# Row factor at the head's output, low weight halves behind the next head's maxima, and filler matmuls in the last expert quad

## The reference, cut to what matters

```python
p = jax.nn.softmax(s, axis=-1)
a = p[:, :, 0] - lam * p[:, :, 1]
o = einsum('bhqk,bkhe->bqhe', a, v)
o = o * lax.rsqrt(jnp.mean(o * o, axis=-1, keepdims=True) + LN_EPS)
```

```python
hid = jax.nn.silu(jnp.einsum('td,edf->tef', t, w1[gi])) * jnp.einsum('td,edf->tef', t, w3[gi])
hid = hid * gate[:, gi, :, None]
out = out + jnp.einsum('tef,efd->td', hid, w2[gi])
```

## Time and profile before

| what | value |
|---|---|
| median of 3 runs | 1187.81 us (1185.96 to 1189.49) |
| profiled execution, its own time | 1190.7 us |
| span of its core | 1188.9 us |
| mean granted clock | 0.974 |
| TensorE matmul busy | 1118.6 us, 94% |
| VectorE busy | 699.5 us, 59% |
| ScalarE busy | 556.3 us, 47% |
| HBM read | 281.87 MB, 239 GB/s over the span |

### The profile page before, as it was taken

How to read it: one execution, slowest core, us unless ns; L and a number is a source line. 1 busy time by engine, 2 the same in 40 slices (tenths; PEclk the granted TensorE clock), 3 DMA queues, 4 the chain that set the end, 5 groups by cost and what they waited for, 6 DMA issues and landing times. The chain is left out here.

```text
span 1188.9 us, 17973 instructions
## 1 busy us (share of the span) xinstructions
PE 1118.6 (94%) x7231; PEld 898.8 (76%) x7231; DVE 699.5 (59%) x1041; ACT 556.3 (47%) x953; POOL 52.4 (4%) x94
## 2 busy tenths in 40 slices
PE   7998899999999999999998999999999999889676
PEld 5987688888789987888887878988887866546333
DVE  3487867778766667778778626745456643312112
ACT  4567556556545646555655424345543322213112
POOL 5000000010000000010000000000000000000000
PEclk9999999999999999999998999999999989979988
DMA  9943378888755333888873652455647799999995
GB/s 273 290 168 104 107 224 295 292 280 292 244 163 191 108 117 130 321 293 275 285 262 100 137 177 72 142 206 180 209 139 262 280 374 369 389 398 386 417 416 225
DMA packets 126510, 285.17 MB, mean 240 GB/s; under 512 B 12222, under 2 KB 72891, under 8 KB 118369
## 3 DMA queue, kind: packets, MB, share of 16 engines
q1 hardware_dynamic: 116512, 249.29, 59.9%
q0 software_dynamic: 9920, 34.80, 9.1%
HBM read 281.87 MB, written 2.20 MB: 239 GB/s over the span
## 5 line engine op out<-in xcount | busy, mean ns | idle before, releaser
L2000 DVE TENSOR_TENSOR w_lo<-ring,w_hi 128x1024 fp32r<-128x1024 f32 (+1 forms) x272 | 320.3, 1212 | 101.1 <-ACT w_hi L1507 91.7
L1507 ACT ACTIVATE w_hi<-ring 128x1024 fp32r<-128x1024 f32 (+1 forms) x272 | 277.0, 1047 | 102.8 <-PE acc L680 77.2
L678 PE MATMUL acc<-w_hi,x_two 128*128 128x512 f32 (+2 forms) x320 | 128.5, 402 | 5.3 <-DVE x_two L1985 4.1
L680 PE MATMUL acc<-w_hi,x_two 128*128 128x512 f32 (+2 forms) x320 | 123.4, 386 | 0.0
L679 PE MATMUL acc<-w_lo,x_two 128*128 128x512 f32 (+2 forms) x320 | 123.3, 385 | 0.0
L678 PE MATMUL pp<-x_two,w_hi 128*128 128x256 f32 x384 | 112.5, 293 | 0.0
L679 PE MATMUL pp<-x_two,w_hi 128*128 128x256 f32 x384 | 108.5, 283 | 0.0
L680 PE MATMUL pp<-x_two,w_lo 128*128 128x256 f32 x384 | 108.5, 283 | 0.0
L678 PE MATMUL acc<-w_hi,hid_hi 128*128 128x512 f32 x256 | 99.8, 390 | 0.0
L680 PE MATMUL acc<-w_hi,hid_lo 128*128 128x512 f32 x256 | 99.6, 389 | 0.0
L679 PE MATMUL acc<-w_lo,hid_hi 128*128 128x512 f32 x256 | 99.6, 389 | 0.0
(11 more groups left out here) (397 smaller groups left out, 2135.4 us busy)
## 6 DMA issues: line engine op xcount, KB each, us to landing
ring<-in_w_up_dram SPq DMA_DIRECT2D x32, 1024.0 KB, 5.7
ring<-in_w_down_dram SPq DMA_DIRECT2D x32, 1024.0 KB, 6.6
exp_ring<-in_w_dram SPq DMA_DIRECT2D x32, 1024.0 KB, 11.3
stage<-in_w_ada_dram POOLq DMA_DIRECT2D x48, 512.0 KB, 6.2
ring<-in_w_in_dram SPq DMA_DIRECT2D x24, 1024.0 KB, 5.3
ring<-in_w_in_a_dram SPq DMA_DIRECT2D x12, 1024.0 KB, 14.2
mod<-in_w_dram SPq DMA_DIRECT2D x19, 512.0 KB, 12.9
ring<-in_w_kv_shared_dram SPq DMA_DIRECT2D x8, 1024.0 KB, 6.2
```

The source lines that it names most:

```text
L678: pe.matmul(out, lhs[0], rhs[0], start=start, stop=False)
L680: return pe.matmul(out, lhs[1], rhs[0], start=False, stop=stop)
L1507: act.activation(shaped(high_half(b, k), raw), raw, ACT.Copy).then_inc(S["hi_ready"], 1)
L2000: dve.tensor_tensor(shaped(low_half(b, k), raw), raw, shaped(high_half(b, k), raw), ALU.subtract).then_inc(S["lo_ready"], 1)
```

## The change

In the last quad TensorE runs five filler matmuls between `up(0)` and the wait for w3. In layer 0 the first map's factor 1/sum is no longer multiplied into the weights: the second map's factor becomes minus lambda times its inverse sum times the first map's sum, and ScalarE's `out` multiplies by the first map's inverse sum, in two instructions (one for each query tile, each with its factor column) where one stood. In both attention layers each `low` of the loop moves behind the next `first`: the low parts of blocks 9 and 11 of a layer move from the end of an iteration to behind the `first` of the next one's even head, those of blocks 8, 10 and 12 from ahead of `first(2i-1)` to behind it. `heads_stat(0, 4)` keeps its place right behind `second(4)`, where `low(12)` no longer stands ahead of it.

```diff
@@ TensorE, experts
                     up(0, lambda e, cols: w1_slots[:, 4 * (s % 2) + e, cols], between=i * 2 + 2).then_inc(S["w1_used"], 1)
+                    if s + 1 == QUADS:
+                        busy(5, turn_bank)
                     pe.wait_ge(w3_in[s % 2], (80 if s % 2 else 64) * (s // 2 + 1))
@@ ScalarE, out(c), layer 0
-                        act.activation(o_tm[:, :, 128 * c:128 * c + 128], head_banks(c)[:, :, 384:512], ACT.Copy)\
-                            .then_inc(S["o_done"], 1)
+                        for q in range(QT):
+                            last = act.activation(o_tm[:, q, 128 * c:128 * c + 128], head_bank(c, q)[:, 384:512],
+                                                  ACT.Identity, scale=rsum[:, c % 2, 2 * q:2 * q + 1])
+                        last.then_inc(S["o_done"], 1)
@@ VectorE, second(c), layer 0
                     for q in range(QT):
                         r1 = rsum[:, b, 2 * q + 1:2 * q + 2]
-                        last = dve.tensor_tensor(r1, r1, lam_s[:, 0:1], ALU.mult)
-                    link(last)
-                    for q in range(QT):
-                        cols = slice(0, 128) if q == 0 else slice(128, 384)
-                        last = dve.tensor_scalar(prob[:, b, 0, cols], prob[:, b, 0, cols],
-                                                 rsum[:, b, 2 * q:2 * q + 1], None, ALU.mult)
+                        last = dve.scalar_tensor_tensor(r1, r1, lam_s[:, 0:1], esum[:, b, 2 * q:2 * q + 1],
+                                                        ALU.mult, ALU.mult)
                     link(last)
@@ VectorE, loop over i of attention
                     first(2 * i - 2)
                     if i >= 2:
+                        low(bl + 5 + 2 * i)
                         out(2 * i - 3)
                     second(2 * i - 2)
-                    low(bl + 6 + 2 * i)
                     if i == 3:
                         heads_stat(0, 4)
                     first(2 * i - 1)
+                    low(bl + 6 + 2 * i)
                     if i == 3:
                         heads_scale(0, 4, 1)
                     keys(i)
                     if i < 3:
                         out(2 * i - 2)
                         second(2 * i - 1)
-                        low(bl + 7 + 2 * i)
                 second(5)
```

## The result

The changed kernel took 1180.95 us (median of 11 runs, 1176.18 to 1183.58) beside 1187.81 for the kernel before (11 runs): 6.9 us less by the medians. The ratio is 0.9938, with a 95% interval from 0.9917 to 0.9960, which is 7.4 us less (4.7 to 9.9). The profiled execution took 1179.81 us with a span of 1178.0, against 1190.7 and 1188.9.

The account below looks back on a forecast made before the run. TensorE, busy for 94% of the span, was taken as the bound, with its stops and half-clock stretches as the losses. Layer 0's 1.8, layer 1's 0 and the fillers' 2.7 us made 4.5 off 1187.81: 1183.3 us, range 1181.0 to 1187.5.

Parts of the forecast that it names:

- The swap: Layer 0, low behind first: scores of head 3 come 1.57 us earlier, those of head 5 2.36 us earlier.
- any wait for w_lo: Sign of being wrong: TensorE waiting anywhere for a low half of the weights.
- rival 4: Blocks 8 to 12, both layers: low halves too late, 1.5 us slower at 0.6 each, 1189.3 us; chance 0.05.
- What is late next: Layer 0: statistics wait for squares, TensorE's stop before o_tm's transposes grows to 2.7 us; turn of head 5 2.03 earlier.
- The end of layer 0: From the turn of head 5 on: ScalarE's tail gives back 0.23 of 2.03 us, leaving 1.8.
- Layer 0's term: Layer 0's attention: 1.8 us gained, with nothing counted for a change in its half-clock stretch.
- rival 1: Layer 0 also loses its half-clock stretch, 1.7 us more: 6.2 us gained, 1181.6 us; chance 0.15.
- Rival 2: Layer 0: the 2.7 us stop brings longer half clock, 1.6 us more; gain 2.9, 1184.9 us; chance 0.15.
- The fillers: Last chunk of the experts: fillers cost nothing in the w3 wait; up(1) at full clock gains 2.7 us.
- Rival 3: One gain does not arrive: layer 0 alone, 1186.0 us, or the fillers' 2.7 alone, 1185.1 us; chance 0.20.
- Layer 1: Layer 1's attention: moved low halves stay hidden, by 1.2 us at block 9; gain and loss 0.
- The sum: Whole kernel: layer 0, layer 1 and the fillers together, 4.5 us less, 1183.3 us.

Follow-up runs that it names:

- e13: The kernel before, unchanged, one more single execution; 1185.2 us.
- e15: The kernel before, unchanged, another single execution; 1182.5 us.
- e12: The changed kernel with ScalarE's squares of head 3 moved ahead of its high halves of block 12; 0.9908 of the kernel before, 1176.95 us.
- e1: The kernel before with the five last-quad fillers alone; ratio 1.0005 to the kernel before.
- e4: The changed kernel without the fillers; ratio 0.9974 to the kernel before.
- e10: The kernel before with the five fillers alone, measured a second time; ratio 0.9971 to the kernel before.
- after: The first profiled execution of the changed kernel; 1179.81 us.
- e7: The changed kernel with the five fillers in the last two quads instead of only the last; ratio 0.9939 to the kernel before.
- e8: The changed kernel again, unaltered, timed in the set of the other experiments; ratio 0.9929 to the kernel before.
- e9: The changed kernel with five filler calls on TensorE ahead of layer 1's loop; ratio 0.9993 to the kernel before.
- e11: The changed kernel without the fillers, measured a second time; ratio 0.9953 to the kernel before.
- e14: The changed kernel, unaltered, one more single execution; 1181.1 us.
- e16: The changed kernel, unaltered, another single execution; 1186.9 us.
- e18: The changed kernel, unaltered, measured a third time; ratio 0.9954 to the kernel before.
- e3: The kernel before with only the row factor moved to the output copy; ratio 0.9974 to the kernel before.
- e17: The changed kernel with head 3's squares ahead of block 12's high halves, measured a second time; ratio 0.9919 to the kernel before.

## Why the prediction was right or wrong

**The swap: right.** 1.57 us before the scores of head 3 were forecast, 1.57 came; the shift at the scores of head 5 was to be 2.36 and was 2.37. The two output copies took 0.61 us (0.65 taken). No wait for a low half appeared where the low halves were moved. The one of 2.7 us ahead of the loop has no moved `low` ahead of it, and e13 and e15, of the kernel before, have it too (1.3 and 1.1 us); so that sign of being wrong ("any wait for w_lo") was drawn too wide, and rival 4 is out.

**What is late next: right.** VectorE's wait for the squares 1.89 (2.1 forecast), TensorE's stop 2.64 (2.7), the turn of head 5 2.05 earlier (2.03). e12 shows the cause by removing it. The last figure is so near because two small misses cancel: the scaling started 0.1 us sooner than forecast, and `second(5)` took 1.25 us, not 1.15. Its two products with one operation more took 0.35 us where the old ones took 0.23: the upper bound of my 0 to 0.1, not the nothing that I took.

**The end of layer 0: mis-sized.** I kept 1.8 of 2.03. At equal clock it is 2.24 (89.60 for e1, 87.36 for e4): the turn of head 7 came 0.8 sooner and ScalarE's tail gave 0.6 back, by the wait [1.4 <-issue] that was 0.7.

**Layer 0's term, with the half-clock stretch left as it is: the step that failed.** The term was 1.8 us of work, and "the half-clock stretch I leave as it is" put the clock's share at 0, from one execution. In the profiled pair it was not 0: layer 0 had its stretch before and none after, and gave 3.5 us where I had 1.8. But the stretch is part of an execution and not of the kernel: the order of before runs without it twice in six, the changed kernel with it three times in five. Over the profiles of the two layouts layer 0 took 90.3 us on average in the old one (before, e1, e10, e13, e15) and 88.0 in the changed one (after, e4, e7, e8, e9, e11, e14, e16, e18). Of these 2.4 us 2.2 are the work at full clock; half clock cost 0.75 us on average in the old layout and 0.6 in the new. So on average the 0 was nearly right, and the work was what the term had too small, by 0.4; that is a part of the miss, and the sum below has the rest as far as it is known. One stretch costs 1.25 us (90.85 against 89.60 in the order of before), where rival 1 put 1.7. Rival 1 (6.2 us, 1181.6) came nearest to the measured median by luck: e8, e16 and e18 fell to half clock in that place. Rival 2's mechanism was seen as well, two stretches on end (6.8 us) in e8 and e18, though layer 0 still took less there than before (89.2 and 89.8 us). The rule from the Trainium skill that I set beside it (TensorE: Matmul & The Clock Gate, "Part 4: PE-mode transpose": transposes do not count as busy time like matmuls) is not settled: after a stop of 2.6 us the same transposes ran at full clock in some executions and at half in others, in after and in e8 for instance.

**The fillers: right in kind, over by a part in the rows.** 2.7 was the profiled execution's price. Seven profiles without fillers took 16.5 to 19.2 us from up(1) to the end, 18.2 on average, the thirteen with fillers 16.5 each: 1.8. I priced one execution and not the spread. Rival 3 (no gain from them) is out: e1 and e10 together lie 2.3 us below the kernel before (standard error 0.6). e7 adds that they arrive only behind the last weights.

**Layer 1: right**, 41.03 us from the scores of head 1 to the transposes of o_tm in every profile.

**The sum.** The stages of single executions give 2.4 + 1.8 = 4.2 us, nearly the 4.5 of the forecast. The timed runs give more: the three measurements of the change lie at 0.9938, 0.9929 and 0.9954, and over all timed runs the mean span fell from 1185.65 (96 runs, standard error 0.3) to 1179.85 (29 runs, 0.5), by 5.8 us, standard error 0.6. On the forecast's scale that is 1182.0, inside the range; that the first median fell below its end is in part the draw of eleven runs, and in part that the range ended only 0.6 us below rival 1.

The granted clock that every timed run has on record says more than the stages. Within the runs of one kernel a clock lower by 0.001 goes with a longer span: by 0.7 us in the kernel before, 0.9 in the changed one, 0.5 to 0.8 in the others with twelve runs or more but for e3's 1.1. The last column is worked out: the work at full clock by the rows, and 0.8 us for each 0.001 above the clock of before.

| kernel | runs | mean clock | mean span below before, us | worked out, us |
|---|---|---|---|---|
| before | 96 | 0.9762 | 0 | 0 |
| fillers alone (e1, e10) | 24 | 0.9795 | 2.3 | 0 + 2.6 |
| change without fillers (e4, e11) | 24 | 0.9773 | 4.3 | 2.2 + 0.9 |
| changed kernel | 29 | 0.9801 | 5.8 | 2.2 + 3.1 |
| squares first (e12, e17) | 12 | 0.9827 | 8.9 | 3.0 + 5.2 |
| delay in layer 1 (e9) | 12 | 0.9778 | 0.3 | -1.7 + 1.3 |

The standard errors of the fourth column are 0.6 to 0.7. So the sum had 1.8 of work where the rows show 2.2, and 2.7 of clock where the runs go with some 3.1; 0.5 us are left. The same account takes most of the other excesses: the squares' 0.8 in the rows against 3.1 in the means, the delay's 3.9 against 5.5. These are averages that go together, not a cause: why an earlier TensorE should be granted more clock later on, and in which stage, no run here isolates, and it stays open. The 1.2 us left over for the change without fillers are the largest remainder.

## What to carry to other kernels

An instruction that only feeds buffers can go behind one that feeds the critical chain, if its own due time leaves the slack; but look at what stood behind it before, because a wait that it had covered (here the statistics for the squares) now holds up the rest of the queue. Price a half-clock stretch as a chance and not as a fixed cost: read several executions before putting it in a sum, and compare the mean granted clock of many timed runs. Here fillers before a wait paid where nothing but TensorE followed; in the quad before, the weight stream took the gain back.

## What the runs showed of the hardware

Half clock behind the same stop differs between executions of the same program: up(1) took 3.6, 5.3, 5.7, 6.05 or 6.3 us in the seven profiles without fillers, three of them of the kernel before (3.6, 6.05 and 6.3). Runs of the kernel before spread with a standard deviation of 2.9 us (0.25%), and the granted clock goes with it: in the first eleven runs of the changed kernel the shortest span (1174.4) had 0.984 and the longest (1181.8) 0.978, a difference of 0.6% in both. The router stretch ran between 0 and 10 us at half clock although TensorE's rows show it busy there. A window of the first profile of before:

```profile
947.00:957.00 10.00, 10.00 (x44) 6.92 (x43) 6.54 (x24) 3.61 (x10) 0.00 (x0) 0.50 1.00 415
```

TensorE busy for all of 10.00 us, at a granted clock of 0.50 (its lower level, 1.2 GHz).
